# A split-float32 transformer kernel: the gate's four tiles move inside the first block's attention, with sigmoid by tanh, heads split one by one, a front with two square buffers and smaller table steps

## What is computed

```python
# state-space half, its gate ("glu")
g = jax.nn.gelu(y)
out = g * jax.nn.sigmoid(g @ w_glu + b_glu)
# attention half: 8 heads
s = jnp.where(mask, (q_nope @ k_nope.T + q_pe @ k_pe.T) * scale, finfo.min)
p = jax.nn.softmax(s)
o = p @ v
# both halves
y = concat([rmsnorm(ya, out_norm_ssm), rmsnorm(yb, out_norm_attn)])
h = h + y @ w_out
```

## Time and profile before

| | |
|---|---|
| median of 3 runs | 3765.52 us (3763.19 to 3766.78) |
| the profiled execution | 3764.26 us, its span 3762.5 us |
| PE, PEld busy | 3632.0 us (97%), 3273.2 us (87%) |
| DVE, ACT, POOL busy | 2426.9 us (65%), 1729.3 us (46%), 280.4 us (7%) |
| granted TensorE clock, mean | 0.981 of full speed |

### The profile page before, as it was taken

How to read it: one execution, slowest core, us unless ns; L and a number is a source line. 1 busy time by engine, 2 the same in 40 slices (tenths; PEclk the granted TensorE clock), 3 DMA queues, 4 the chain that set the end, 5 groups by cost and what they waited for, 6 DMA issues and landing times. The chain is left out here.

```text
span 3762.5 us, 56571 instructions
## 1 busy us (share of the span) xinstructions
PE 3632.0 (97%) x23326; PEld 3273.2 (87%) x23326; DVE 2426.9 (65%) x3603; ACT 1729.3 (46%) x2283; POOL 280.4 (7%) x316
## 2 busy tenths in 40 slices
PE   6979999999999999999999999999999999999998
PEld 5977989899998988998888888889889988888887
DVE  7864666566566665556766767766555577576676
ACT  4434444344344444445544535543444455454453
POOL 4840000000000210001000000021000100000000
PEclk8988999999999999999999999999999999999999
DMA  4221445555555454343555555545433355555554
GB/s 162 101 71 46 155 177 184 188 183 179 191 186 186 149 185 142 129 160 127 189 187 184 187 188 185 188 151 181 160 135 135 125 192 186 190 182 182 194 178 152
DMA packets 90944, 616.46 MB, mean 164 GB/s; under 512 B 10048, under 2 KB 12864, under 8 KB 33344
## 3 DMA queue, kind: packets, MB, share of 16 engines
q1 hardware_dynamic: 90688, 612.85, 45.8%
HBM read 610.72 MB, written 2.10 MB: 163 GB/s over the span
## 5 line engine op out<-in xcount | busy, mean ns | idle before, releaser
L2313 DVE TENSOR_TENSOR wlo<-raw,whi 128x2048 fp32r<-128x2048 f32 (+3 forms) x421 | 923.3, 2193 | 296.5 <-ACT whi L2133 293.7
L1849 PE MATMUL gemm<-x_pair,whi 128*128 128x512 f32 x2816 | 1006.2, 402 | 9.0 <-DVE x_pair L2478 5.1
L2133 ACT CAST whi<-raw 128x2048 fp32r<-128x2048 f32 (+3 forms) x422 | 767.1, 1820 | 271.2 <-DMA raw<-in_stream_dram 271.2
L1850 PE MATMUL gemm<-x_pair,wlo 128*128 128x256 f32 x2816 | 792.2, 281 | 0.0
L1849 PEld LDWEIGHTS gemm<-x_pair,whi 128*128 128x128 f32 x2816 | 531.1, 189 | 141.7 <-issue 5.4
L1850 PEld LDWEIGHTS gemm<-x_pair,wlo 128*128 128x128 f32 x2816 | 533.8, 190 | 1.0
L1849 PE MATMUL gemm<-f_pair,whi 128*128 128x512 f32 x1408 | 497.7, 399 | 0.0
L1516 DVE TENSOR_TENSOR wlo<-raw,whi 128x2048 fp32r<-128x2048 f32 (+2 forms) x153 | 339.3, 2218 | 86.9 <-ACT whi L1421 86.5
L1850 PE MATMUL gemm<-f_pair,wlo 128*128 128x256 f32 x1408 | 395.4, 281 | 0.0
L1421 ACT CAST whi<-raw 128x2048 fp32r<-128x2048 f32 (+2 forms) x154 | 283.7, 1843 | 99.0 <-DMA raw<-in_stream_dram 98.9
L1849 PEld LDWEIGHTS gemm<-f_pair,whi 128*128 128x128 f32 x1408 | 264.6, 188 | 66.1
(11 more groups left out here) (520 smaller groups left out, 7157.6 us busy)
## 6 DMA issues: line engine op xcount, KB each, us to landing
raw<-in_stream_dram SPq DMA_DIRECT2D x446, 1024.0 KB, 4.8
raw<-in_stream_dram SPq DMA_DIRECT2D x96, 896.0 KB, 4.5
raw<-in_stream_dram SPq DMA_DIRECT2D x32, 768.0 KB, 4.1
raw<-in_stream_dram SPq DMA_DIRECT2D x16, 960.0 KB, 4.6
raw<-in_stream_dram SPq DMA_DIRECT2D x4, 952.0 KB, 4.6
xT<-in_hT_dram SPq DMA_DIRECT2D x4, 544.0 KB, 9.8
xT<-in_hT_dram SPq DMA_DIRECT2D x1, 2176.0 KB, 8.7
out_dram<-xT SPq DMA_DIRECT2D x3, 512.0 KB, 2.9
```

The source lines that it names most:

```text
L1849: pe.matmul(both, whi[:, slot(n), k * P:k * P + P], pairs[:, :, c, :], start=(k == 0), stop=False, skip_group_check=True)
L1850: return pe.matmul(bank(use)[:, 0:T2], wlo[:, slot(n), k * P:k * P + P], pairs[:, 0, c, :], start=False, stop=(k == nk - 1), skip_group_ch ...
L2133: act.copy(whi[:, slot(n), 0:wide], raw[:, slot(n), 0:wide]).then_inc(w_hi, 1)
L2313: dve.tensor_tensor(wlo[:, slot(n), 0:wide], raw[:, slot(n), 0:wide], whi[:, slot(n), 0:wide].bitcast(F32), ALU.subtract).then_inc(w_lo, 1)
```

## The change

It does the following.

- **Front, input**: `sq0` is two buffers of eight slots, so ACT no longer waits for `sum_x`. PE starts with tile 0 alone for the first eight rows of chunks, then takes tile 1. The sines are computed after the first weight split, `factors()` comes after the twelfth `low`, and `b_powers(0)` before the first evacuation.
- **Front, tables**: POOL builds the first half of the rotation table in one piece; DVE builds the second half in the pieces of `LATE_SPANS`, behind tiles 1, 2, 3, 5 and 7, the largest step cut in two.
- **Front, order**: at tile 14 `keep_taps(5)` comes before and `b_powers(6)` behind the splits of the latents; POOL's five rotary products come before `back(6)` and `c_powers(7)`; DVE's `side(18)` lies between the third and the fourth rotary piece.
- **Attention**: the probabilities are scaled in place and then transposed by `pe.transpose`; the diagonal matrix is gone, here and in the two later layers.
- **Gate**: its four tiles lie in attention steps 12 to 23, a third of a tile in each, on the two PSUM banks G[2] and G[3]. Sigmoid is written as half of 1 + tanh(x/2): DVE forms u * (1 + tanh), and the norm's small number is 4 * EPS, so that the factor 2 drops out. Heads are split and squared one by one, seven of them in the steps of `ATTN_AT`, and their squares are added on DVE, so that one matmul sums them.
- The weight tiles 20 to 25 are split inside the attention, and tiles 24 to 27 are loaded there.

```diff
-SPANS = [(2 ** j, min(2 ** j, J1 - 2 ** j)) for j in range(7)]
+SPANS = [(j, 2 ** j, 0, min(2 ** j, J1 - 2 ** j)) for j in range(7)]
+LATE_SPANS = [*SPANS[:3], SPANS[6], *SPANS[3:5], (5, 32, 0, 16), (5, 48, 16, 16)]
+LATE_AT = {1: (0, 3), 2: (3, 4), 3: (4, 6), 5: (6, 7), 7: (7, 8)}
+GLU_AT = 12
+ATTN_AT = (12, 13, 14, 16, 19, 22, 25)
...
             def _(pool):
-                rotations(pool, 1, tmp_late, late_part, late_to)
-                pool.wait_ge(early_to, len(SPANS) + 1)
+                pool.wait_ge(x_summed, 8)
+                rotations(pool, 0, tmp_early, early_part, early_to, SPANS)
...
-                    if c == 7:
+                    if c == 6:
                         pool.wait_ge(made, 12)
...
             def _(pe):
                 for n in range(2):
                     pe.wait_ge(w_lo, n + 1)
-                for c in range(DC):
+                    for c in range(8):
+                        pe.wait_ge(x_low, c + 1)
+                        in_step(n, c)
+                for c in range(8, DC):
...
-                    pe.wait_ge(diag, u + 1)
+                    pe.wait_ge(normed, u + 1)
...
-                        m = pe.matmul(A[2 + u % 2][0:n, j * 128:j * 128 + nq], Pr[0:nq, u % 3, k0:k0 + n], dg[0:nq, u % 2, 0:nq],
-                                      start=True, stop=True)
+                        m = pe.transpose(A[2 + u % 2][0:n, j * 128:j * 128 + nq], Pr[0:nq, u % 3, k0:k0 + n], ident(nq))
...
+                def glu(t, part):
+                    n = NB + t
+                    if part == 0:
+                        pe.wait_ge(w_lo, n + 1)
+                        if t == 0:
+                            pe.wait_ge(vp_kept, 8)
+                            pe.wait_ge(y_copied, 2)
+                        else:
+                            pe.wait_ge(gated, 2 * t)
+                    for k in (range(0, 3), range(3, 6), range(6, 8))[part]:
...
+                            m = step3(G[2 + e][:, 0:TK], whi[:, slot(n), at], wlo[:, slot(n), at], op1[:, 0, k, :], op1[:, 1, k, :], k == 0, k == 7)
...
                     if s in LATE:
                         side(20 + LATE.index(s))
+                    if 0 <= s - GLU_AT < 12:
+                        glu(*divmod(s - GLU_AT, 3))
...
             def _(act):
+                    if s == GLU_AT:
+                        act.wait_ge(y_copied, 2)
+                        for c in (6, 7):
+                            act.activation(u1[:, c, keep], u1[:, c, keep], ACT.Gelu_apprx_tanh).then_inc(g_made, 1)
...
+                    if s in (5, 9, 18, 21):
+                        hi(22 + (5, 9, 18, 21).index(s))
+                    if s >= GLU_AT + 3 and (s - GLU_AT) % 3 == 0 and s <= GLU_AT + 12:
+                        gates((s - GLU_AT) // 3 - 1)
+                    if s in ATTN_AT:
+                        attn_high(ATTN_AT.index(s))
...
             def _(dve):
-                lo(20)
-                lo(21)
...
+                    if s in (9, 13, 16, 19, 22, 25):
+                        lo(20 + (9, 13, 16, 19, 22, 25).index(s))
...
 ...
                 for k in range(8):
                     pe.wait_ge(s_low, k + 1)
                     for t in range(2):
                         m = out_step(t, k)
                         if k == 7:
                             m.then_inc(w_used, 1)
+                    sum_s(k)
```

More of the change, by code:

```diff
@@ L143, in back_plan @@
     plan, uses, banks = [], {}, 0
-    for kind, count, each in (("glu", TILES1["glu"], 2), ("w_out", TILES1["w_out"], 2)):
+    for kind, count, each in (("glu", TILES1["glu"], 0), ("w_out", TILES1["w_out"], 2)):
         for k in range(count):
@@ L386, in build, with rotations @@
         turn = lambda a, j, h, w: trig[:, a, 3 + j, 16 * h:16 * h + 16].unsqueeze(2).to_broadcast([P, 16, w])
-        def rotations(eng, h, tmp, part, level, first=0, last=len(SPANS)):
+        def rotations(eng, h, tmp, part, level, spans, first=0, last=len(SPANS)):
             cos, sin = (tab[:, a, 16 * h:16 * h + 16, :] for a in range(2))
@@ L467, in _ @@
                 sp.dma_start(xT[:, :, :], ins["hT"].rearrange("p (c t) -> p c t", c=DC)).then_inc(reloaded, 16)
+                for n in range(NB + RAW, NB + 4 + RAW):
+                    load(n)
+                b.issued = NB + 4 + RAW
                 sp.wait_ge(reloaded, 16)
@@ L564, in sum_x @@
                     pe.wait_ge(x_paired, c + 1)
[L565 removed]
+                    pe.matmul(A[0][:, 0:T1], cst("ones", 128), sq0[c // 4][:, 2 * c % 8, :], start=(c == 0), stop=(c == 7)).then_inc(x_summed, 1)
                 def taps(c):
@@ L1115, in _ @@
                         lo(0)
+                    if c == 7:
                         lo(1)
+                    if c == 11:
+                        factors()
                 lo(2)
+                b_powers(0)
                 invert(rstd0[:, :], 1)
@@ L1135, in _ @@
                     if n == 14:
+                        keep_taps(5)
                         for c in range(4):
                             latent(c)
-                    side(n)
+                        b_powers(6)
+                    else:
+                        side(n)
+                    if n in LATE_AT:
+                        rotations(dve, 1, tmp_late, late_part, late_to, LATE_SPANS, *LATE_AT[n])
                 for i in range(3):
```

267 lines of the change are left out of this document (124 added, 143 removed).

## The result

The changed kernel takes 3736.65 us in the median of 7 runs (3724.86 to 3739.95), the kernel before 3764.58 us in the median of 7 (3748.97 to 3766.78). The ratio is 0.9923, with a 95% interval from 0.9907 to 0.9939: 28 us faster. The forecast was 3729, so the 36.7 us that it expected were 9 us too much. The profiled execution of the changed kernel took 3726.59 us, its span 3724.8, 37.7 us less than the 3762.5 before.

The account below looks back on a forecast made before the run. PE was taken as the bound after 393 us (97% busy), with waits in every stage before; 14 - 1.8 + 4.5 + 5 + 15 = 36.7 us off 3764.3 gave 3729 in the medians' frame, 8-in-10 range 3706 to 3748.

Parts of the forecast that it names:

- the rival of the slow clock: Attention: steps 7 to 11 run at 1.2 GHz and cost 8 to 12 us more, 3737 to 3741; chance 0.20.
- start, up to the first taps: Front: PE opens with tile 0 alone and the wait for tile 4's split goes; gain 14 us, bounds 3 to 17.
- from there to turn_u after tile 14: Front, to 182 us: PE was already full, so the start's gain of 14 us is kept whole.
- tile 14: Front: DVE waits for the taps of chunk 5 before splitting the latents; loss 1.8 us, 0 to 3.
- rotary step: Front: rotary products first remove PE's 6.3 us wait, but the values' evacuation comes late; gain 4.5 us, 2 to 10.
- attention and gate to w_out's third tile: First block: 34.8 us go and 29.7 come; gain 5 us, from a loss of 8 to a gain of 16.
- later layers' attention: Later layers: 136 diagonal matmuls save 0.137 us each, less growing waits for ACT's copies; gain 15 us, 8 to 20.
- the rival on the start: Front: DVE's splits beside POOL's tables lengthen and the start gains 3 us instead of 14; 3746 to 3759, chance 0.10.
- The transposes: First block's attention: plain transposes replace diagonal matmuls, six in each of 8 heads; 10 us saved in all.
- the gate's waits: Attention steps 15, 18 and 21: gate tiles wait for their banks 1.9, 3.6 and 3.6 us, 9.1 in sum.
- clock column 1.0 from step 12: Attention: sign that the forecast holds, PE's clock being full from step 12 once the gate's matmuls fill PE.
- the clock is 0.5 for more than 10 us inside the attention: Attention: sign that the forecast is wrong, PE at half clock there for over 10 us.

Follow-up runs that it names:

- experiment 3: Kernel before with only the transposes changed (probabilities scaled in place, plain transposes, first block and both later layers): 3722.24 us, ratio 0.9883.
- experiment 10: Kernel before, unchanged, run again for the pace of its later feed-forward stages: 3749.36 us.
- 11: Kernel before, unchanged, run a third time for the pace of its later feed-forward stages: 3751.45 us.
- 2: Changed kernel with ACT's tanh pair ahead of the weight split in attention steps 18 and 21: 3721.74 us, one run.
- 5: Changed kernel with attention chunks 13 to 15 of w_out's first two tiles behind the state-space half and its sums: 3734.04 us, one run.
- experiment 6: Changed kernel with ACT's tanh pair ahead of the exponential in attention steps 15, 18, 21 and 24: 3712.83 us, one run.
- Experiment 1: Changed kernel with DVE's two large rotation-table pieces at tiles 5 and 7 ahead of the state-space mixer's half step: 3723.46 us, ratio 0.9895.
- Experiment 7: Kernel of Experiment 1 with factors() and b_powers(0) behind the evacuation of tile 1 again: 3740.96 us, one run.
- Experiment 4: Changed kernel with POOL's c_powers(7) behind the second rotary product instead of after all five and back(6): 3732.04 us, one run.
- experiment 9: Kernel of 8 with the 256-column table piece of tile 3 moved behind keep_taps(0) and b_powers(1) of tile 4: 3703.3 us, ratio 0.9851.
- 8: Changed kernel with table pieces in DVE's gap, c_powers(7) in POOL's gap, tanh first, w_out chunks 13 to 15 behind the sums: 3694.03 us, ratio 0.9838.

## Why the prediction was right, and where it was not

The time lies in the range and the sign was right; the size was 9 us too large. The median of 3736.65 us lies at the edge of what the rival of the slow clock gave (3737 to 3741), but it did not come about that rival's way. By the terms of the sum, from the two profiled executions:

| term | forecast | measured |
|---|---|---|
| start, up to the first taps | 14 | 11.6 (67.75 for 79.31) |
| from there to turn_u after tile 14 | kept whole | 9.8 lost (187.07 for 188.85) |
| tile 14 | -1.8 | -1.7 (the wait for the latents ends at 197.11 for 197.18) |
| rotary step | 4.5 | 3.9 (first scores 264.44 for 268.40) |
| attention and gate to w_out's third tile | 5 | 5.6 |
| feed-forward net's start | none | -2.2 |
| later layers' attention | 15 | 18.4, without the pace |
| sum | 36.7 | 25.8 |

Each measured value is the difference of two executions. Over four traces of the front of before (before, 3, 10, 11) and four of the changed front (changed, 2, 5, 6) the terms spread like this: the start wins 10.3 to 12.5 us, the stretch behind it loses 9.8 to 12.4, tile 14 loses 1.7 in all of them, the rotary step wins 2.8 to 3.9. The first scores are 2.2 us earlier in the mean (265.1 for 267.3), not 4.0. So of the 16.7 us forecast for the front 2 to 4 came.

**The start** itself won less because PE's waits between tile 0 and the first taps were 10.5 us, 6.6 of them for `tap_blocks`, where 7 had been left. The step that failed is "From there to 182 us PE was already full, so the gain is kept whole." PE was full because DVE and POOL were not late; the change took that away by putting two pieces of the table behind tiles 5 and 7. The text had DVE's work as "only reordered" for the stretch before 63 us and did not cost the pieces behind it. It had the right price at hand in the rival on the start (a split beside POOL's tables takes 3.23 instead of 2.29 us), but placed it before the first taps. Experiment 1 showed it: the same operations moved by a few rows give back 10.6 us by `turn_u` after tile 14. Experiment 7 showed the first half of the term, that the factors' place is worth 9.5 us.

**Tile 14 and the rotary step** came as worked out. The values' evacuation began at 252.6 us, where 251.5 was the estimate for the end of `c_powers(7)`, and PE's wait was 5.1 us for a forecast of 4. Experiment 4 showed the cause by taking it away.

**Attention and gate** are right in sum, and in parts as far as they were tried. The transposes won 9.8 us for 10 (experiment 3). The rest cost 4.2 us for 4.9. The waits were forecast at 1.9, 3.6 and 3.6 us and measured at 1.6, 3.4 and 3.4, and w_out's third tile waited 5.5 for 5.8. What was too small is what a gate wait costs behind it: the sum had 9.1 us for all of the gate's waits, and experiment 6 won 13.4 by removing them, because 5 us of slow clock went too. Since the sum was right nevertheless, something else was taken too high as a cost or too low as a gain; which, was not tried. One candidate is seen: the wait of 5.5 us fell to 0.6 as forecast, and the half clock at the attention's start lasted 17 us instead of 24, which the sum did not count. DVE's scaling stayed hidden, as expected, though its pieces have 80, 208 and 272 columns and not 128 to 256: PE waited 0.9 us for it, once.

**The rival of the slow clock** wanted steps 7 to 11 at 1.2 GHz. They ran from 284.5 to 293.9 us in the changed kernel, and the clock was 1.00:

```profile
283.70:293.90 10.20, 9.29 (x59) 6.16 (x57) 7.41 (x29) 6.32 (x21) 0.00 (x0) 1.00 0.01 2
```

With plain transposes in place of all diagonal matmuls of that attention it was 1.00 from 290 to 320 us in experiment 3 too. The rule that transposes do not count as PE being busy (the Trainium skill, TensorE: Matmul & The Clock Gate, Part 4: PE-mode transpose) was cited for it. In this attention, where scores and values lie between the transposes, the traces do not bear it out. Whether a stretch of transposes alone would lower the clock no run here shows.

Two of the prediction's signs on the clock failed. "clock column 1.0 from step 12" did not come true: around step 12 and around the end of both waits of 3.39 us the clock was at half, for 6.8 us each time. And by the sign "the clock is 0.5 for more than 10 us inside the attention" the forecast would be wrong: it was 0.50 from 266.6 to 283.7 us. But the kernel before had 24 us of it there, so that sign could not tell the two cases apart, and only a slow clock beyond that of before costs anything in the sum.

**The table loads** of step 12 cost what the row of before said. ACT's timeline of the changed kernel:

```profile
297.76 0.42 ACT L975 ACTIVATE probs_t<-att 128x128 f32<-128x128 f32 x2
298.19 1.28 ACT L1011 ACT_TABLE_LOAD   x1
299.49 0.72 ACT L1011 ACTIVATE u<-u 128x258 f32<-128x258 f32 x2
```

From the copies' end at 298.18 to the gelu at 299.49 is 1.3 us, and PE had no wait over 1 us in steps 12 to 14. The drain that the Trainium skill adds (ScalarE: Activation LUTs, What ACT_TABLE_LOAD costs) is not seen in this place.

**The feed-forward net's start.** A wait of 2.9 us for the last input chunk lies there before and after. Behind it the clock was 1.00 in the kernel before and 0.83 in the changed one, in the 10 us from 485 us on; the lead falls from 9.6 us to 7.4. In experiment 3 nothing was lost there. But it is not a matter of the kernel alone: in experiment 10, the kernel before once more, the clock behind the same wait of 2.9 us is 0.83 as well (492.2 to 502.2 us). This was not in the sum.

**The later layers** won 18.4 us for 15 (37.7 at the end, less the 7.4 of the first block and the 11.9 of the pace). In the ten traces that have these layers the same gain, read from the 176th split of a weight tile to the end without the pace, is 16.7 to 21.2 us, and the two further traces of the kernel before differ from its first by 0.7 and 2.2. So the term was too small in all of them. The waits for ACT's copies grew by 5.3 us (16.9 for 11.6), more than the 3.6 that were taken off; other waits shrank by about 1. What was too small is the saving of one transpose, 0.137 us. In one round of the first later layer, with four of them and no wait, the kernel before takes 11.66 us (1500.09 to 1511.75) and the changed one 10.87 (1489.38 to 1500.25), 0.20 each. How the rest adds up was not tried.

## What to carry to other kernels

Before a gain at the start is carried to the end, look at what the change puts on every engine behind it: a stretch in which PE is full says only that the others were in time until now. A piece of work that may run anywhere belongs ahead of the next wait of its engine, not behind the work that ends the wait: the same six rows of the table took 4.9 us of DVE in one place, with PE waiting behind them, and 2.2 us in the other, inside a wait of DVE (experiment 1). And a part that looks like a detail should be tried alone: here the transposes alone gained more than the whole change (experiment 3). On an engine that feeds the matmuls, the short operation that PE needs goes ahead of the long one that only the next tile needs (tanh before exponential, copies and split: 13 us).

## What the runs showed that was not expected

- Two alternating matmuls of 512 and 256 columns, in a stretch where PE has no gap and the clock reads 1.00, take 353 ns together in one execution and 346 in another, for a whole feed-forward stage of some 700 us, or 12 us. It changes from one execution to the next, stage by stage. What sets it is open.
- A wait costs more than its length. The three gate waits, 8.4 us, were worth 13.4. But the same wait of the same kernel does not cost the same each time: 2.9 us at the feed-forward net's start of the kernel before had a clock of 0.83 behind it in experiment 10 and 1.00 in the first trace, and 2.71 us in a later layer a slow clock in experiment 9 and not in 8. So a wait's price in clock can't be read from its length alone.
- While POOL multiplies, an operation of DVE on 256 columns of both tables took 0.99 us instead of 0.42, and a weight split 2.85 instead of 2.26 to 2.29.
